# Two transformer blocks on one core: ScalarE's gate functions placed one turn later, decay's exponential too, and the forget gate's affine step behind another group

## The reference

```python
proj = h @ w_in            # q_a, k_a, v_a, q_h, f_h, i_h, g_h, gate_a, gate_h
y_a  = sliding_window_attention(qa, ka, va, sinks) @ w_attn_proj
# HGRN2 recurrence, 8 heads of 128, chunks of 64
f    = lb + (1 - lb) * sigmoid(f_h);  key = 1 - f
q    = silu(q_h);  b = cumsum(log f) within a chunk
o_h  = recurrence(q, key, exp of differences of b, i_h)   # the "decay" factors
o_h  = rmsnorm(o_h, hg_norm)
y_h  = (o_h * sigmoid(g_h)) @ w_hgrn_proj
merged = sigmoid(gate_a) * y_a + sigmoid(gate_h) * y_h
x = x + gate1 * rmsnorm(merged @ w_out, g_post_mix)
```

## Time and profile before

| what | us |
|---|---|
| median of 3 runs | 2767.49 (2767.38 to 2768.65) |
| the profiled execution | 2764.63 |
| its span, first to last instruction | 2762.9 |
| PE busy in the span | 2605.7 (94%) |
| DVE busy | 1823.1 (66%) |
| ACT busy | 1317.8 (48%) |
| job hg (three turns, from the first turn's transposes to the last's) | 183.27 |
| job m1 (three turns, from head to head) | 124.48 |
| job gh (three turns, from head to head) | 93.55 |

### The profile page before, as it was taken

The page is one execution under the profiler, slowest core; times in us unless marked ns, Lnnn a source line. Parts: engine busy times, 40 slices in busy tenths (PEclk is TensorE's granted clock), DMA queues, the critical chain, the costliest instruction groups (busy, mean ns, idle before and its releaser), DMA issues.

```text
span 2762.9 us, 42044 instructions
## 1 busy us (share of the span) xinstructions
PE 2605.7 (94%) x15018; PEld 2258.5 (82%) x15018; DVE 1823.1 (66%) x2222; ACT 1317.8 (48%) x1704; POOL 31.1 (1%) x36
## 2 busy tenths in 40 slices
PE   4889898999898999999999998999999999999997
PEld 4777777887787788888888886888888888888886
DVE  6878887776677655577555555556567775477764
ACT  1435554555543544443444445555555554455542
POOL 0000000000000000000000000012000000000000
PEclk8799998999999999999999998999999999999999
DMA  9888884454485566699666554554555566555564
GB/s 374 318 288 268 267 280 134 144 160 130 148 273 188 147 187 183 188 304 303 188 189 184 182 180 125 183 153 145 175 160 184 188 189 197 186 183 182 182 198 137
DMA packets 491945, 550.70 MB, mean 199 GB/s; under 512 B 18777, under 2 KB 448865, under 8 KB 491841
## 3 DMA queue, kind: packets, MB, share of 16 engines
q1 hardware_dynamic: 489840, 542.10, 61.3%
q0 software_dynamic: 2000, 7.22, 0.8%
HBM read 547.14 MB, written 2.11 MB: 199 GB/s over the span
## 4 chain that ended last, share of the span: by engine, by line
PE 77%; DVE 10%; issue 6%; ACT 4%; DMA 1%; SPq 1%; DVEq 0%; ACTq 0%; POOL 0%
PE psg L1781 72%; PE pss L1781 5%; DVE w_lo L1152 2%; ACT w_hi L657 2%; DVE gate_acc_mix L1133 1%; DVE first_acc L1230 1%; SPq L521 1%; DMA raw<-in_w_in 1%; DMA stage<-in_w_ada 0%; DVE proj L1116 0%; DVE decay L1348 0%; DVE Pq L1360 0%; DMA raw<-in_w_out 0%; DVE decay L1362 0%; DVE decay L1349 0%
## 5 line engine op out<-in xcount | busy, mean ns | idle before, releaser
L1781 PE MATMUL psg<-X,w_hi 128*128 128x512 f32 x4512 | 1612.8, 403 | 31.3 <-issue 14.7
L1152 DVE TENSOR_TENSOR w_lo<-raw,w_hi 128x1024 fp32r<-128x1024 f32 x832 | 1008.3, 1228 | 724.3 <-ACT w_hi L657 713.9
L657 ACT ACTIVATE w_hi<-raw 128x1024 fp32r<-128x1024 f32 x832 | 865.1, 1056 | 863.5 <-PE psg L1781 842.1
L1781 PE MATMUL psg<-X,w_lo 128*128 128x256 f32 x4512 | 1252.3, 283 | 0.0
L1781 PEld LDWEIGHTS psg<-X,w_hi 128*128 128x128 f32 x4512 | 850.8, 190 | 231.8 <-issue 23.5
L1781 PEld LDWEIGHTS psg<-X,w_lo 128*128 128x128 f32 x4512 | 862.8, 191 | 13.9 <-issue 1.4
L1781 PE MATMUL psg<-hid,w_hi 128*128 128x512 f32 x1664 | 584.7, 395 | 0.2 <-issue 0.2
L1781 PE MATMUL psg<-hid,w_lo 128*128 128x256 f32 x1664 | 458.1, 279 | 0.0
L1781 PEld LDWEIGHTS psg<-hid,w_hi 128*128 128x128 f32 x1664 | 309.5, 188 | 71.2 <-issue 0.6
L1781 PEld LDWEIGHTS psg<-hid,w_lo 128*128 128x128 f32 x1664 | 312.1, 188 | 3.9
L642 ACT ACTIVATE half<-psg 128x512 f32<-128x512 f32 x205 | 119.2, 581 | 10.1 <-PE psg L1781 10.1
(11 more groups left out here) (298 smaller groups left out, 1603.5 us busy)
## 6 DMA issues: line engine op xcount, KB each, us to landing
raw<-in_w_in SPq DMA_DIRECT2D x212, 512.0 KB, 4.2
raw<-in_w_ffn_in SPq DMA_DIRECT2D x176, 512.0 KB, 4.1
raw<-in_w_up SPq DMA_DIRECT2D x176, 512.0 KB, 4.9
raw<-in_w_ffn_out SPq DMA_DIRECT2D x88, 512.0 KB, 4.5
raw<-in_w_down SPq DMA_DIRECT2D x88, 512.0 KB, 4.6
gate_w_mix<-in_w_ada SPq DMA_DIRECT2D x160, 256.0 KB, 5.0
stage<-in_w_ada SPq DMA_DIRECT2D x64, 512.0 KB, 10.5
raw<-in_w_out SPq DMA_DIRECT2D x64, 512.0 KB, 3.6
```

Source lines behind the costliest of these rows:

```text
L657: nc.scalar.activation(w_hi[:, half_slot(j, p), :, :], raw[:, slot_of(j, p), :, :], ACT.Copy).then_inc(hi_ready, 1)
L1152: nc.vector.tensor_tensor(w_lo[:, hs, :, :], raw[:, slot_of(j, p), :, :], w_hi[:, hs, :, :].bitcast(F32), ALU.subtract).then_inc(raw_used, 1)
L1781: return nc.tensor.matmul(out_, l, r_, start=start, stop=stop)
```

## The change

On ACT, in jobs hg, m1 and gh the functions that followed a group end are moved into `side`. They now run behind the `w_hi` copy of the next chunk: at 4 and 8 and, for a turn's last group, at 0 of the next turn (behind the loop for the last turn). In m1 they stand at 4 and 10. In m1 and gh the exponential of `decay` moves from 3 to 4, ahead of the sigmoid there. On DVE the affine step of the forget gate moves from behind group 1 to behind group 2 (the third of four). The first turns of hg and gh are written out apart from the loop (`peel`). Behind the last turn of gh, `head_rstd` and `head_high` now come ahead of the last sigmoid.

```diff
                 if p == 3:
                     act.wait_ge(SH["m"], h + 1)
                     nc.scalar.activation(s_next[CH:P, :, :], s_in[CH:P, :, :], ACT.Copy).then_inc(SH["mo"], 1)
-                    if not ends:
-                        head_decay(h + 1)
+                if p == 4 and not ends:
+                    head_decay(h + 1)
...
+                def gate_function(i, g):
+                    act.wait_ge(ps_free, sums_done(J["hg"], i, g))
+                    apart()
+                    t = heads4[:, ds(2 * i, 2), g, :]
+                    nc.scalar.activation(t, t, ACT.Silu if g == 0 else ACT.Sigmoid).then_inc(SH["act"], 1)
+
                 def side(b, p, final):
 
+                    if p == 0 and not is_first(b):
+                        gate_function(b - 1, 3)
+                    if p == 4:
+                        gate_function(b, 0)
+                    if p == 8:
+                        gate_function(b, 1)
                     if p == 9 and final:
                         head_inputs(0)
...
-                def after(i, g):
-                    if g == 2:
-                        return
-                    act.wait_ge(ps_free, sums_done(J["hg"], i, g))
-                    apart()
-                    t = heads4[:, ds(2 * i, 2), g, :]
-                    nc.scalar.activation(t, t, ACT.Silu if g == 0 else ACT.Sigmoid).then_inc(SH["act"], 1)
-                job(J["hg"], after, side)
+                job(J["hg"], None, side, None, True)
+                gate_function(J["hg"].iters - 1, 3)
...
-                def after(i, g):
-                    if g % 2 == 0:
+                def side(i, p, final):
+                    head_side(i, p, is_first(i), False)
+                    if p in (4, 10):
+                        g = 0 if p == 4 else 2
                         act.wait_ge(ps_free, sums_done(J["m1"], i, g))
                         apart()
                         sigmoid(proj[:, ds(4 * i + g, 2), :], 2 * i + g // 2)
-                job(J["m1"], after, lambda i, p, final: head_side(i, p, is_first(i), False), peel=True)
+                job(J["m1"], None, side, peel=True)
             if runs("gh"):
-                def after(i, g):
+                def gate_sigmoid(i, g):
                     act.wait_ge(ps_free, sums_done(J["gh"], i, g))
                     apart()
                     sigmoid(proj[:, ds(4 * i + 2 * g + DT, 2), :], 2 * i + g + 8)
-                job(J["gh"], after, lambda i, p, final: head_side(i + 4, p, False, final))
+
+                def side(i, p, final):
+                    head_side(i + 4, p, False, final)
+                    if p == 0 and not is_first(i):
+                        gate_sigmoid(i - 1, 1)
+                    if p == 4:
+                        gate_sigmoid(i, 0)
+                job(J["gh"], None, side, None, True)
                 head_rstd(HGH - 1)
                 head_high(HGH - 1)
+                gate_sigmoid(J["gh"].iters - 1, 1)
...
                 def after(i, g):
-                    if g == 1:
+                    if g == 2:
 
                         dve.wait_ge(SH["act"], 3 * i + 2)
```

## The result

| | before | changed |
|---|---|---|
| median of four runs each | 2767.62 | 2722.99 (2722.83 to 2723.93) |
| ratio, 95% interval | | 0.9839 (0.9822 to 0.9856) |
| profiled execution; its span | 2764.63; 2762.9 | 2723.09; 2721.2 |

The kernel is 44.6 us faster. Forecast were 2727.5 (range 2715 to 2749), so the direction, the range and most of the size were right, and the gain was 4.6 us larger than the 40.0 of the sum.

What follows compares the result with a forecast made beforehand. With PE busy for 94% of the span and DVE the late engine in hg, gains of 20.0 (hg), 6.9 (m1), 9.9 (gh) and 3.2 us (end of gh) sum to 40.0, giving 2727.5 us, range 2715 to 2749.

Steps and rivals of the forecast that it cites:

- The rival of the transfers: hg: transfers take over and set the turn, so hg gains nothing; 20.0 us in all, 2747.5; chance 12%.
- The turn of hg: hg: a turn takes 55.5 us instead of 61.1, counted from DVE's own pace; three turns gain 16.8 us.
- The 0.7 us for chunk 1: hg: added to each turn because step 1's high half now stands behind the sigmoid of the previous turn's last group.
- from M to step 5: hg: from the end of the `mod` result (M) to the low half of step 5, over PE's scores, 6.4 us.
- The three holes of 8.8 us: hg: DVE stands 3.23, 3.11 and 2.43 us a turn waiting for ACT; the change takes all three away.
- 47.6 us of waits in all: hg, m1, gh and the start of wh: total of PE's waits before the change, none for a transfer.
- `probs_t`: Last turn of hg: PE's 3.2 us wait stays and grows, but ends as early as DVE does.
- m1: m1: three turns gain 6.9 us, 3.8 of PE's idle time and 3.1 of clock; bounds 0 and 8.0.
- the prediction's other reading: m1: the clock's 3.1 us may stay lost although the waits go; the sum would be 36.9 us.
- gh: gh: the `o_sq` waits all go; three turns gain 9.9 us, including 1.9 of clock; bounds 0 and 10.3.
- The check value for failure: gh: if `r_c` waits grow above 1 us, the exponential's new place costs what the sigmoid's gave.
- The end of gh: Last head to wh's second chunk: an earlier `head_rstd` gains 3.2 us of a 5.0 us wait; bounds 0 and 5.0.

Runs made afterwards that it cites:

- e6: Changed kernel with hg's accumulating gate steps on half of their columns (`mod` incomplete, transfers the same): 2714.43 us, ratio to before 0.9805.
- e8: Changed kernel with hg's `mod` result taken by DVE ahead of the low half of chunk 3 instead of behind it: 2719.56 us, ratio to before 0.9826.
- e1: Kernel before with only the hg part (ACT's functions one chunk later, affine step behind group 2): 2746.55 us, ratio to before 0.9928.
- e4: Kernel before with only the affine step moved behind group 2 in hg: 2767.73 us, ratio to before 1.0004.
- e9: Changed kernel with ACT's copy of `probs_t` ahead of decay's first exponential in hg's last turn: 2720.96 us, ratio to before 0.9838.
- e5: Changed kernel with decay's exponential back at 3, ahead of the copy of the group's sum: 2732.04 us, ratio to before 0.9869.
- e2: Kernel before with only the m1 and gh part (sigmoids, decay's exponential, last head ahead of last sigmoid): 2748.13 us, ratio to before 0.9934.
- e10: Changed kernel with the edits of e8 and e9, and m1's first chunk ahead of the wait for `attn_x`: 2715.17 us, ratio to before 0.9818.

## Why the prediction was right, and where its sizes were off

- **Who bounds hg.** Right: DVE is the late engine, and with less work for it PE's own turn comes out (e6). Not all of it is work: 1.1 us a turn are the order of its steps (e8). The rival of the transfers is excluded by e6, at 319 GB/s against the 303 that it doubted.
- **The turn of hg.** The count gave 54.9 and I added 0.6 "for handovers that I can't see". Measured 54.7 in e1 and in the changed kernel. That was 2.4 us too much in three turns, 1.8 of them the added term, and nearly half of the 5.3 us by which the stretches exceed the sum. The 0.7 us for chunk 1 and the wait of 1.4 at the scores came out (0.72; 4.0 in the last three turns). So did the two large terms: from M to step 5 6.7 us (counted: 6.4), the rest of the turn 47.4 (counted: 47.8, of which 7.6 were an estimate).
- **The three holes of 8.8 us.** They are gone at their places, as the text said, but 0.72 and 2.08 us stand one chunk behind two of them, so the turn fell by 6.4 us and not by 8.8. The count had both, the 0.7 by name and the other in its first term, the way over PE's scores. Nor are the holes a list of separate gains: with the affine step moved alone, its wait turns into one for the high half (e4).
- **"47.6 us of waits in all".** Two rows of the same view are not in that sum: `w_lo` with 0.7 us, and `attn_x` with 4.5 (shown in e9). The change left the latter at 4.5 us, and the end of hg hangs on it, as e9 shows.
- **`probs_t`.** Right that it stays, grows and ends as DVE's `head_begin` lets it, here over ACT's exponential, which stands ahead of the copy (e9): 12.66 us from the transposes to the product with v against 12.65 before, its wait 5.6 instead of 3.2.
- **m1.** 7.1 us against 6.9; the clock's share came back whole (1.00 here, and three turns of 117.1 to 117.4 us in all seven profiles without the bank waits), so the 3.1 us that the prediction's other reading let stay were not left. That reading came from the Trainium skill, "TensorE: Matmul & The Clock Gate", Part 1, by which the moment of the clock's change depends on a window that runs free of the kernel. Of this the traces do show a sign: behind the same three bank waits the clock fell twice before the change, three times in e1 and once in e5. The first turn of m1, which I gave nothing, gained 1.0 us.
- **gh.** 9.5 against 9.9; `r_c` waits at most 0.4 us, where the text had 0.2. The check value for failure, 1 us, was not reached.
- **The end of gh.** The chain was right (3.3 against 3.2). What the sum lacked is the clock behind the wait, 2.0 us. The bound of 5.0 lacked it too: that is the wait alone, and the two parts make 5.3.
- **Added code on ACT.** No sign of a cost: m1 and gh stretches of e1 and e2 are equal to the kernels that they are taken from within 0.5 us. The written-out turns were not timed by themselves.

ACT at the last head, on which the end of gh rests. Before, `o_rs` started at 727.93, behind the sigmoid, 4.2 us after the half copy's start at 723.74; after, 0.48 us after it:

```profile
687.32 0.58 ACT L642 ACTIVATE half<-psg 128x512 f32<-128x512 f32 x1
687.80 0.47 ACT L793 ACTIVATE o_rs<-pss,eps_col 128x256 f32<-128x256 f32 x1
```

## What to carry to other kernels

Where one engine feeds a stream and also serves the results of that stream, try the stream's next piece ahead of the steps that wait for the other engine; the step then waits in time that nobody wants. Sum an engine's steps round one turn of the loop and lay the result beside the other engines' sums: that gave the new turn to 0.2 us here, and an allowance on top of it only did harm. Test edits to one hole both alone and together, since a wait with two causes behind one another shows only the later one. And measure such an edit past the point that it moves: in e10 the stretch that was looked at became shorter and the next one longer by more.

## What was not expected of the hardware

The length of one wait does not tell whether the granted clock falls behind it. A bank wait in m1 before the change, with the 10 us behind it, then the same wait in e5:

```profile
541.56 0.50 PE L1781 MATMUL psg<-X,w_hi 128*128 128x512 f32 x1 [1.22 <-DVE proj L1116]
541.56:551.56 10.00, 10.00 (x48) 8.70 (x49) 6.69 (x8) 6.94 (x10) 0.00 (x0) 0.83 0.40 130
```
```profile
521.52 0.49 PE L1797 MATMUL psg<-X,w_hi 128*128 128x512 f32 x1 [1.24 <-DVE proj L1132]
521.52:531.52 10.00, 10.00 (x56) 8.74 (x57) 7.67 (x11) 6.81 (x10) 0.00 (x0) 1.00 0.40 130
```

The clock was 0.83 behind the one and 1.00 behind the other. The kernel before has such a pair in hg: the mask products took 1.44 us behind a wait of 2.27 and 0.81 behind one of 2.26. At the start of wh, though, the outcome was the same each time: 1.00 behind 1.7 us in seven profiles, 0.74 to 0.88 behind 4.9 or 5.0 in five.

The start of hg is reached through nearly the same instructions in all twelve profiles (e8 and e10 move one step there), and still lay between 193.46 and 200.34 us. It goes with the clock. PE waits for the rotated keys (`kr`) at about 155 us, 3.48 us in the changed kernel and 3.50 in e8. From 160 to 170 us, first the changed kernel, then e8:

```profile
160.00:170.00 10.00, 10.00 (x46) 8.55 (x45) 3.81 (x6) 3.70 (x7) 0.00 (x0) 0.76 0.48 154
```
```profile
160.00:170.00 10.00, 10.00 (x58) 8.78 (x57) 6.82 (x10) 4.76 (x8) 0.00 (x0) 0.97 0.72 231
```

The three profiles with the highest clock in these 10 us (0.96 to 0.98) reach the scores first (193.46 to 195.03), the three with the lowest (0.73) last (198.24 to 200.34). That the clock sets the rest of the spread as well is not shown. With differences of a few us, that start has to be taken out before two profiles are compared.
